# An encoder step on one core: diagonal blocks of 128 columns, a rotary part in another place, and column products in groups of 512, 512 and 128 frames

## What is computed

```python
def mla_queries(x, pos, w_in, q_norm_g, w_uq, w_uk):
    proj = jnp.einsum('btd,de->bte', x, w_in)          # 512 latent + 2048 gate columns
    cq = rms_norm(proj[..., :Q_LORA], q_norm_g)
    gate = proj[..., Q_LORA:]
    q = jnp.einsum('btr,re->bte', cq, w_uq)            # per head 128 plain + 64 rotary
    ...
    q_rope = rope(q[..., NOPE_DIM:], pos)

def attend_prompt(...):                                # queries in blocks of 128
    mask = key_chunk[None, :] <= q_chunk[:, None]      # chunks of 64 frames, causal
    p = softmax(where(mask, scores * ATTN_SCALE, -1e30))
    o = (p @ c) @ w_uv
```

## Time and profile before

| | us |
|---|---|
| median of 3 runs | 1947.16 (1946.81 to 1948.17) |
| the profiled execution | 1946.45 |
| its span in the trace | 1944.3 |
| TensorE busy | 1914.9 (98%) |
| weight loads busy | 1808.9 (93%) |
| VectorE busy | 1061.8 (55%) |
| ScalarE busy | 768.6 (40%) |
| GpSimd busy | 394.0 (20%) |

### The profile page before, as it was taken

How to read it: one execution, slowest core, us unless ns; L and a number is a source line. 1 busy time by engine, 2 the same in 40 slices (tenths; PEclk the granted TensorE clock), 3 DMA queues, 4 the chain that set the end, 5 groups by cost and what they waited for, 6 DMA issues and landing times.

```text
span 1944.3 us, 31501 instructions
## 1 busy us (share of the span) xinstructions
PE 1914.9 (98%) x11771; PEld 1808.9 (93%) x11771; DVE 1061.8 (55%) x1943; ACT 768.6 (40%) x1346; POOL 394.0 (20%) x322
## 2 busy tenths in 40 slices
PE   9999999999999999999999999999999999999998
PEld 8999999999987999999999999999999989988886
DVE  4355446445658612422466676666666677753632
ACT  4333233233422221211455555555555567761100
POOL 0221222122311010000042432432433410000000
PEclk9999999999999999999999999999999999999999
DMA  6121122022236412233211112111111243363421
GB/s 183 34 78 55 35 67 78 27 62 68 79 117 201 128 44 69 80 107 104 89 34 50 41 50 63 34 54 56 38 49 42 73 135 92 96 226 136 157 87 43
DMA packets 186082, 158.55 MB, mean 82 GB/s; under 512 B 36144, under 2 KB 170544, under 8 KB 185744
## 3 DMA queue, kind: packets, MB, share of 16 engines
q1 hardware_dynamic: 180784, 139.60, 23.7%
q10 hardware_dynamic: 5040, 17.37, 2.6%
q0 software_dynamic: 176, 0.43, 0.1%
HBM read 115.52 MB, written 41.84 MB: 81 GB/s over the span
## 4 chain that ended last, share of the span: by engine, by line
PE 54%; DVE 7%; issue 5%; ACT 3%; DMA 1%; DVEq 0%; ACTq 0%; SPq 0%
PE ps L115 16%; PE ps L117 16%; PE ps L116 16%; PE ps L1925 1%; PE ps L1908 1%; PE ps L1907 1%; DVE h_pt_l L109 1%; ACT h_p L2041 1%; ACT h_p L2030 1%; DVE s_mx L2801 1%; DVE h_mx L2169 1%; DVE h_p L2126 1%; DVE h_p L2131 1%; DMA m_g_raw<-scratch_o 1%; DVE h_gate L2191 0%
## 5 line engine op out<-in xcount | busy, mean ns | idle before, releaser
L1821 POOL TENSOR_SCALAR h_p<-h_p,h_rsum 128x128 f32<-128x128 f32 (+7 forms) x128 | 220.7, 1725 | 442.8 <-DVE h_rsum L2173 442.8
L115 PE MATMUL ps<-act_h,a_w_l 128*128 128x384 f32 x768 | 270.8, 353 | 1.7 <-DVE a_w_l L109 1.7
L117 PE MATMUL ps<-act_h,a_w_h 128*128 128x384 f32 x768 | 260.1, 339 | 0.0
L116 PE MATMUL ps<-act_l,a_w_h 128*128 128x384 f32 x768 | 259.9, 338 | 0.0
L115 PE MATMUL ps<-act_h,m_c_l 128*128 128x384 f32 x480 | 162.9, 339 | 0.0
L117 PE MATMUL ps<-act_h,m_c_h 128*128 128x384 f32 x480 | 162.5, 339 | 0.0
L116 PE MATMUL ps<-act_l,m_c_h 128*128 128x384 f32 x480 | 162.5, 339 | 0.0
L115 PEld LDWEIGHTS ps<-act_h,a_w_l 128*128 128x128 f32 x768 | 144.2, 188 | 6.5 <-issue 3.3
L116 PEld LDWEIGHTS ps<-act_l,a_w_h 128*128 128x128 f32 x768 | 144.4, 188 | 3.3 <-issue 3.3
L117 PEld LDWEIGHTS ps<-act_h,a_w_h 128*128 128x128 f32 x768 | 144.1, 188 | 0.0
L104 ACT ACTIVATE h_pt_h<-ps 128x128 fp32r<-128x128 f32 (+2 forms) x192 | 87.1, 490 | 108.7 <-PE ps L1925 108.5
(11 more groups left out here) (322 smaller groups left out, 4817.5 us busy)
## 6 DMA issues: line engine op xcount, KB each, us to landing
a_w_raw<-in_w_in_a SPq DMA_DIRECT2D x31, 512.0 KB, 4.1
m_c_raw<-in_w_in_b SPq DMA_DIRECT2D x20, 512.0 KB, 4.3
scratch_gate<-m_sg SPq DMA_DIRECT2D x16, 576.0 KB, 5.3
o_w_raw<-in_w_out_b SPq DMA_DIRECT2D x16, 512.0 KB, 6.3
h_gate<-scratch_gate SPq DMA_DIRECT2D x62, 128.0 KB, 2.0
scratch_og<-h_gate SPq DMA_DIRECT2D x62, 128.0 KB, 1.7
o_g_raw<-scratch_og SPq DMA_DIRECT2D x24, 256.0 KB, 4.3
a_xn<-in_x SPq DMA_DIRECT2D x9, 512.0 KB, 4.5
```

The costliest lines, as they stand in the source:

```text
L115: nc.tensor.matmul(out, ll, rh, start=first, stop=False)
L116: nc.tensor.matmul(out, lh, rl, start=False, stop=False)
L117: return nc.tensor.matmul(out, lh, rh, start=False, stop=last)
L1821: nc.gpsimd.tensor_scalar(weights_of(u), weights_of(u), rsum[:, u % PB], None, ALU.mult).then_inc(S["p_ready"], 1)
```

## The change

- A new helper, `products_beside`, issues the three steps of several products side by side: the first step of each, then the second of each, then the third. `columns` takes several (tile, group) pairs and uses it. The groups are now frames 0 to 511, 512 to 1023 and 1024 to 1151, in one bank each, and ScalarE and VectorE read a tile as 1152 columns in a row.
- A tile does group 0 alone and then groups 1 and 2 beside each other. The first two tiles do (1,0), (0,0), the last frame tile's turning, (0,1), and then (1,1), (0,2), (1,2) beside each other, with both counts of `c_done` at the end. The waits on `tl_done` ask for more frame tiles.
- Scores of block 0 are 128 columns wide. Values go through the key blocks from place 1 on, with place 0 last and only over the second half of the queries. The zeroing and its wait are gone.
- In the first pair R2 stands behind V0 on TensorE, in bank 7; its cosine stands before the first maximum, its four copies before exp 1, its sine and sums behind the second maximum, and its reading by ScalarE behind V3.

```diff
+def products_beside(nc, parts, first, last):
+    for term in range(3):
+        for out, (lh, ll), (rh, rl) in parts:
+            mm = nc.tensor.matmul(out, lh if term else ll, rl if term == 1 else rh,
+                                  start=first and term == 0, stop=last and term == 2)
+    return mm
...
-        return bank[:, 3 * (i % 2):3 * (i % 2) + 3, 0:TG]
+        return flat(bank[:, 3 * (i % 2):3 * (i % 2) + 3])[:, 0:T]
...
-        def columns(i, tg):
-
-            cols = slice(tg * TG, (tg + 1) * TG)
+        def columns(*blocks):
+
             for kt in range(KD):
-                mm = product(nc, pc(i)[:, tg], (c_h[:, i % 2, kt], c_l[:, i % 2, kt]),
-                             (k.act_h[:, kt, cols], k.act_l[:, kt, cols]), kt == 0, kt == KD - 1)
-            if tg == NTG - 1:
-                mm.then_inc(c_done, 1)
+                parts = []
+                for i, tg in blocks:
+                    cols = slice(tg * BANK, min(tg * BANK + BANK, T))
+                    parts.append((pc(i)[:, cols], (c_h[:, i % 2, kt], c_l[:, i % 2, kt]),
+                                  (k.act_h[:, kt, cols], k.act_l[:, kt, cols])))
+                mm = products_beside(nc, parts, kt == 0, kt == KD - 1)
+            return mm
...
-        pe.wait_ge(tl_done, 4)
-        columns(1, 0)
+        pe.wait_ge(tl_done, 5)
+        columns((1, 0))
         pe.wait_ge(sum_done, 9)
-        columns(0, 0)
+        columns((0, 0))
         turn_tile(NT - 1)
-        pe.wait_ge(tl_done, 7)
-        columns(0, 1)
+        pe.wait_ge(tl_done, NT)
+        columns((0, 1))
         pe.wait_ge(tl_done, NT + 1)
-        columns(0, 2)
-        columns(1, 1)
-        columns(1, 2)
+        columns((1, 1), (0, 2), (1, 2)).then_inc(c_done, 2)
...
-            for tg in range(NTG):
-                columns(i, tg)
+            columns((i, 0))
+            columns((i, 1), (i, 2)).then_inc(c_done, 1)
...
-FIRST_PROJ = ["R0", "R1", "QA0", "QA1", "KA0", "KA1", "QA2", "R2"] + PROJ[8:]
+FIRST_PROJ = ["R0", "R1", "QA0", "QA1", "KA0", "KA1", "QA2", "UT", "V0", "R2"] + PROJ[10:]
...
-            n = max(GQ, P * (qb + 1))
+            n = P * (qb + 1)
...
-            for i in range(nb):
+            order = [*range(1, nb), 0]
+            for i in order:
                 b, cols = nb - 1 - i, slice(e * P, e * P + P)
-                mm = product(nc, value_out(G), (v_h[:, b, cols], v_l[:, b, cols]),
-                             (pt_h[G % 2][:, i], pt_l[G % 2][:, i]), i == 0, i == nb - 1)
+                q = slice(0 if i else P, GQ)
+                mm = product(nc, value_out(G)[:, q], (v_h[:, b, cols], v_l[:, b, cols]),
+                             (pt_h[G % 2][:, i, q], pt_l[G % 2][:, i, q]), i == 1, i == order[-1])
...
-        for x in (pt_h[0], pt_h[1], pt_l[0], pt_l[1]):
-            nc.scalar.activation(x[:, 0, 0:P], k.ident[:], ACT.Identity, scale=0.0).then_inc(S["zeroed"], 1)
-        shift(0, 2, True)
```

More of the change, by code:

```diff
@@ L1384, in column_tile @@
                 dst = sums[:] if i == 0 else sg[:, i % 2]
-                nc.scalar.activation(dst.rearrange("p (a b) -> p a b", a=3), pc(i), ACT.Square)
-                nc.scalar.copy(cq_raw[:, i].rearrange("p (a b) -> p a b", a=3), pc(i)).then_inc(cq_out, 1)
+                nc.scalar.activation(dst, pc(i), ACT.Square)
+                nc.scalar.copy(cq_raw[:, i], pc(i)).then_inc(cq_out, 1)
             else:
@@ L1392, in column_tile @@
                     act.wait_ge(gate_stored[j % 2], 16 * (j // 2))
-                nc.scalar.activation(sg[:, j % 2].rearrange("p (a b) -> p a b", a=3), pc(i), ACT.Sigmoid).then_inc(sig_done, 1)
+                nc.scalar.activation(sg[:, j % 2], pc(i), ACT.Sigmoid).then_inc(sig_done, 1)
             if i + 2 < NCOL:
@@ L1506, in column_tile @@
                 j = i - NCQ
-                at = sg[:, j % 2].rearrange("p (a b) -> p a b", a=3)
+                at = sg[:, j % 2]
                 dve.wait_ge(sig_done, j + 1)
@@ L1625 @@
 PLACE = {"R1": 0, "R2": 2, "V0": 3, "V1": 4, "V2": 5, "V3": 6}
-FIRST_PLACE = {"R0": 6, "QA0": 5, "KA0": 2, "KA1": 3, "QA2": 4}
-FIRST_PROJ = ["R0", "R1", "QA0", "QA1", "KA0", "KA1", "QA2", "R2"] + PROJ[8:]
+FIRST_PLACE = {"R2": 7, "R0": 6, "QA0": 5, "KA0": 2, "KA1": 3, "QA2": 4}
+FIRST_PROJ = ["R0", "R1", "QA0", "QA1", "KA0", "KA1", "QA2", "UT", "V0", "R2"] + PROJ[10:]
 HIGH_COUNT = {s: sum(x[0] != "R" for x in PROJ[:i + 1]) for i, s in enumerate(PROJ)}
@@ L1690, in heads_programs @@
     bank = k.bank
-    names = ("uq_loaded ukv_loaded zeroed wh_ready wl_ready table_loaded proj_done proj_high proj_out rope_cos rope_moved rope_sin rope_sum rq_high rq_out s_done masked max_done "
+    names = ("uq_loaded ukv_loaded wh_ready wl_ready table_loaded proj_done proj_high proj_out rope_cos rope_moved rope_sin rope_sum rq_high rq_out s_done masked max_done "
              "exp_done inv_done scale_go p_ready t_done t_high t_out pv_done o_out ql_stored qr_stored qs_ready").split()
@@ L1883, in proj, with scores @@
             mm.then_inc(S["proj_done"], 1)
-        def scores(pr, u):
+        def scores(pr, u, first=False):
             e, qb, g = place_of(u)
             if u < 2:
-                pe.wait_ge(S["proj_out"], pr * NP + STEP[("R1", "V0")[u]] + 1)
+                pe.wait_ge(S["proj_out"], pr * NP + (STEP["R1"] if u == 0 else step_of("V0", first)) + 1)
             else:
@@ L1938, in values @@
             nb = 2 * (g + 1)
-            for i in range(nb):
+            order = [*range(1, nb), 0]
+            for i in order:
                 b, cols = nb - 1 - i, slice(e * P, e * P + P)
-                mm = product(nc, value_out(G), (v_h[:, b, cols], v_l[:, b, cols]),
-                             (pt_h[G % 2][:, i], pt_l[G % 2][:, i]), i == 0, i == nb - 1)
+                q = slice(0 if i else P, GQ)
+                mm = product(nc, value_out(G)[:, q], (v_h[:, b, cols], v_l[:, b, cols]),
+                             (pt_h[G % 2][:, i, q], pt_l[G % 2][:, i, q]), i == 1, i == order[-1])
             mm.then_inc(S["pv_done"], 1)
-        for s in FIRST_PROJ[:8]:
+        for s in FIRST_PROJ[:7]:
             proj(0, s, True)
-        pe.wait_ge(S["zeroed"], 4)
         def body(pr, first, last):
-            for s in ("UT", "V0"):
+            for s in ("UT", "V0", "R2") if first else ("UT", "V0"):
                 proj(pr, s, first)
@@ L1953, in body @@
             proj(pr, "V1", first)
-            scores(pr, 1)
+            scores(pr, 1, first)
             for s in ("V2", "V3"):
@@ L2071, in beside @@
                     k.samples.first_keys_high(act, u - KEYS_FROM)
-            for s in ("UT", "V0", "R2"):
+            for s in ("UT", "V0") if first else ("UT", "V0", "R2"):
                 proj(pr, s, first)
@@ L2076, in body @@
             proj(pr, "V1", first)
+            if first:
+                shift(pr, 2, first)
             exp(pr, 1)
-            for s in ("V2", "V3"):
+            for s in ("V2", "V3", "R2") if first else ("V2", "V3"):
                 proj(pr, s, first)
@@ L2203, in _ @@
             proj(0, s, True)
-        cosines(0, 2, True)
-        sines(0, 2)
         def body(pr, first, last):
+            if first:
+                dve.wait_ge(S["proj_out"], step_of("UT", first))
             for s in ("UT", "V0"):
                 proj(pr, s, first)
+            if first:
+                cosines(pr, 2, first)
             largest(pr, 0)
@@ L2212, in body @@
             largest(pr, 1)
+            if first:
+                sines(pr, 2)
             proj(pr, "V2", first)
```

## The result

| | before | after |
|---|---|---|
| median of the runs, us | 1947.5 (1946.8 to 1948.2) | 1976.4 (1975.0 to 1976.9) |
| ratio | | 1.0149 (1.0136 to 1.0161) |
| the profiled execution | 1946.45 | 1976.93 |
| its span | 1944.3 | 1975.1 |

The change costs 28.9 us. The forecast was +22.6, to 1969.8, with a range of 1934 to 1978.

The account below looks back on a forecast made before the run. TensorE, busy 98% of the span, was taken as the bound. Terms -2.7 + 18.9 + 6.3 + 1.5 - 1.4 = +22.6 us on 1946.45 gave 1969.1, as a median 1969.8; range 1934 to 1978.

Parts of the forecast that it names:

- Pitch of narrow products: Column tiles: a 128 column product costs a load's pace, 110 ns, so three widths take 570 ns against 530.7: +18.9 us.
- Rival 1: Narrow products run at their columns' pace, 64 ns, if weights load further ahead: -12.0 us, 1935; chance 0.14.
- rival 2: Narrow rounded products are taken like full f32 ones, 2 x 112 = 224 ns: +108 us, 2055; chance 0.18.
- The joint end: First two column tiles ended together: the chain for tile 2's weights is bare, TensorE waits at cl_ready 3, +6.3 us.
- The clock behind it: Lower clock level after TensorE's wait at the joint end of the first two tiles: +1.5 us, bounds 0 and 2.
- Narrow blocks: Values of place 0 and scores of query block 0: 272 products at 110 instead of 120 ns, -2.7 us.
- The rotary part: First pair, R2 moved behind V0: TensorE's 1.36 us stand before scores 1 goes, -1.4 us.
- Sum: All terms of the likeliest case: +22.6 us on the profiled 1946.45 us, 1969.1; median of the runs 1969.8.
- this case: The likeliest case, narrow products at a load's pace with the joint end's stall: 1969.8, own range 1961 to 1977; chance 0.60.

## Why the forecast held, step by step

- **Pitch of narrow products.** Right, and it was the step that decided the sign. A rounded product of 128 columns costs one load. I took 110 ns for it and 230 for 512 columns; the step of the two is 343, with 233 for the wide one, so the narrow one is between 110 and 112, as the one column products showed. The term is 480 x 45.8 ns = 22.0 us and not 18.9, just above the end that I gave (21.8; 480 x 45.3 is 21.7). Rival 1 (64 ns) and rival 2 (224 ns) are out by the kernels with narrow products in a row and with 192 columns. A load is never more than one product ahead: of the 11771 loads in the trace of before, and of the 11771 in that of the changed kernel, none starts over 0.025 us ahead of the product before its own. The Trainium skill (TensorE: Matmul & The Clock Gate, table at its head) gives TensorE a window of 64 from which weight loads are pulled ahead of products in flight; no trace here shows a load that is pulled further ahead than one product.
- **The joint end.** 6.3 us forecast, 6.2 measured, by the same chain, and it goes where tile 0 is ended first. The second load beside it cost nothing.
- **The clock behind it.** 1.5 us taken, 2.3 shown; my upper bound of 2 was too low, because the first products of the kernel, from which it came, were at the lower level for 3.8 us and these for 5.3.
- **Low clock behind the sums of squares.** Not forecast. 1.6 us in the changed kernel: eight products of 512 columns at 0.43 in the window from 740 to 745. I looked for idle time only.
- **Narrow blocks.** -2.7 forecast, -2.0 in the trace. That this is near 272 x (112 - 120) ns = -2.2 us is luck: TensorE is busy 3.9 us less, and 1.9 us of new idle time take half of it back. That moving them "changes no wait" was wrong: the waits for h_gate grow by 1.0 us, and those for h_v_l by 1.6.
- **The rotary part.** -1.4 forecast; the wait of 1.36 us is gone and 0.2 us came. Right by the trace of the waits; by time the two kernels with and without it are 1.7 us apart, within the noise of both, and from the first scores to the last value product their two profiles differ by 0.8.
- **Sum.** -2.0 + 22.0 + 6.2 + 2.3 + 1.6 - 1.2 = +28.9 us. The traces give the same by stages: +32.4 for the column stage, where the sum has 32.1, and -3.4 from the first scores to the last value product (607.1 us before, 603.7 after), where it has -3.2. That the sum meets the medians to the tenth is luck, since the ratio's interval allows 26 to 31 us. The profiled spans differ by 30.8; the rest is a low stretch near 598 us (below), which the profile of before does not have.

So the direction and the two largest mechanisms were forecast, and the size was not: +22.6 was 6.3 us short, 3.1 of it in the pitch, 1.6 in the clock behind the sums of squares, 0.8 in the clock behind the wait and 0.9 in the heads, with 0.1 the other way at the joint end. The measured 1976.4 lies at the upper end of the 1961 to 1977 that I gave for this case, and the stated range is wide because it also holds a faster kernel.

## What to carry to other kernels

Before a group is cut, compare its columns with one weight load: below the width at which the two are equal (here 112 ns, between 192 and 256 columns) a product gets no cheaper, and what its neighbours take over is paid in full. Putting short and long products side by side does not pool their time, since only one load is ahead. And where the counts of two buffers are joined, look for the chain that hung on the earlier one; its length less the work left in front of the waiter is the stall. Last, work taken off the engine that bounds the kernel brings less than its own time where another engine is close behind: here 3.9 us less work in the heads brought 2.0.

## What the runs showed of the hardware

The granted clock fell to its lower level in places where TensorE had not been idle: behind 24 narrow and 18 one column products (from 731 to 738 us, in the kernel whose groups do not stand beside each other), and behind the one column products of the changed kernel. It did not fall there in before, whose products ahead of them have 384 columns, but neither did it in the kernel with tile 0 ended first, where they have 512 and 128. So the widths alone do not decide it.

It is not the same in each execution of the same code. TensorE waits 2.4 to 2.8 us for m_x near 595 us in each kernel, with code that no kernel here changes. In the profile of before the clock stays full behind it; in the first profile of the changed kernel it does not, and in the second it does. Before, and the changed kernel's first:

```profile
597.63 0.40 PE L116 MATMUL ps<-m_w_l,m_g_h 128*128 128x512 f32 x1
597.86 0.40 PE L117 MATMUL ps<-m_w_h,m_g_h 128*128 128x512 f32 x1
```

```profile
597.80 0.63 PE L116 MATMUL ps<-m_w_l,m_g_h 128*128 128x512 f32 x1
598.22 0.63 PE L117 MATMUL ps<-m_w_h,m_g_h 128*128 128x512 f32 x1
```

Of the eleven profiles the low stretch stands there in seven. In the changed kernel's the granted clock is 0.68 from 597 to 599 us and 0.65 from 599 to 602, which is worth some 1.7 us. That is as much as some of the differences looked for here, and is a reason to compare stages and not spans.
